# Modulation rows of the first layer's stages: pairs of tiles into one PSUM result

## The reference

```
mod_x = (silu(c) @ w_ada[l] + b_ada[l])[:, None, :]
mod_c =  silu(c_ctx) @ w_ada[l] + b_ada[l]
sh1, sc1, gate1, sh2, sc2, gate2 = split(mod_x, 6)
hx = rms_norm(x, norm_g[l, 0]) * (1.0 + sc1) + sh1     # used from the start of the layer
...                                                     # gate1 .. gate2 are used late in it
```

## Time and profile before

| | us |
|---|---|
| median of the runs (3) | 3360.63 |
| lowest and highest | 3359.15, 3364.89 |
| span of the profiled execution | 3357.8 |
| PE busy in the span | 3114.1 |
| DVE, ACT, POOL busy | 1500.2, 1162.7, 831.6 |

### The profile page before, as it was taken

One profiled execution on the slowest core, in us unless ns is written; L12 is line 12 of the kernel. 1 busy time (PEld: TensorE's weight loads), 2 busy tenths in 40 slices (PEclk: granted clock), 3 DMA queues, 4 the chain that ended last, 5 costly groups with the idle time before them and its releaser, 6 DMA issues.

```text
span 3357.8 us, 79208 instructions
## 1 busy us (share of the span) xinstructions
PE 3114.1 (93%) x34382; PEld 2493.0 (74%) x34382; DVE 1500.2 (45%) x2358; ACT 1162.7 (35%) x2403; POOL 831.6 (25%) x518
## 2 busy tenths in 40 slices
PE   7999898999999998999999888989899989989998
PEld 5777676778777786888888666767667667768886
DVE  4455473745444653100144464756565456330033
ACT  4433333423334424211112353434333345342222
POOL 2211111111123132222223221111111243434453
PEclk9999999999999999999999989999999999999999
DMA  5424242434454441111111233413233343522222
GB/s 212 135 97 145 81 142 101 130 121 144 145 166 151 158 169 57 51 63 62 62 50 63 75 101 98 127 63 120 65 122 106 93 140 115 188 69 95 99 88 75
DMA packets 246714, 364.56 MB, mean 109 GB/s; under 512 B 154080, under 2 KB 155376, under 8 KB 245904
## 3 DMA queue, kind: packets, MB, share of 16 engines
q1 hardware_dynamic: 226976, 294.57, 27.6%
q10 hardware_dynamic: 14976, 35.66, 2.7%
q0 software_dynamic: 4464, 29.92, 2.5%
HBM read 290.88 MB, written 69.21 MB: 107 GB/s over the span
## 4 chain that ended last, share of the span: by engine, by line
PE 76%; DVE 6%; issue 5%; ACT 4%; DMA 2%; DVEq 2%; POOLq 2%; PEld 1%; SPq 1%; POOL 0%; PEldq 0%; ACTq 0%
PE banks L281 20%; PE banks L282 18%; PE banks L283 18%; PE banks L1684 2%; PE banks L1023 2%; PE banks L1695 1%; PE banks L1648 1%; PE banks L395 1%; PE banks L1687 1%; PE banks L1745 1%; POOLq L2430 1%; DVE arena L597 1%; PE banks L2057 1%; PE banks L1051 1%; DMA arena<-chunk_inputs 1%
## 5 line engine op out<-in xcount | busy, mean ns | idle before, releaser
L283 PE MATMUL banks<-hx_rounded,slot_rounded 128*128 128x512 f32 (+1 forms) x1624 | 575.1, 354 | 0.0
L906 POOL TENSOR_TENSOR slot_rounded<-slot,branch_weights_high 128x512 fp32r<-128x512 f32 x188 | 251.4, 1357 | 1286.2 <-ACT branch_weights_high L901 1284.9
L281 PE MATMUL banks<-hx_high,weight_parts 128*128 128x512 f32 (+1 forms) x1512 | 537.9, 356 | 10.9 <-DVE hx_low L545 10.4
L281 PE MATMUL banks<-hx_rounded,branch_weights_high 128*128 128x512 f32 (+1 forms) x1280 | 498.8, 390 | 48.1 <-DVE arena L1364 8.6
L282 PE MATMUL banks<-hx_low,weight_parts 128*128 128x512 f32 (+1 forms) x1512 | 538.0, 356 | 0.0
L283 PE MATMUL banks<-hx_high,weight_parts 128*128 128x512 f32 (+1 forms) x1512 | 535.9, 354 | 0.0
L282 PE MATMUL banks<-resid_rounded,branch_weights_high 128*128 128x512 f32 (+1 forms) x1280 | 452.7, 354 | 0.0
L283 PEld LDWEIGHTS banks<-hx_rounded,slot_rounded 128*128 128x128 f32 x1624 | 312.2, 192 | 44.3
L281 PEld LDWEIGHTS banks<-hx_rounded,branch_weights_high 128*128 128x128 f32 x1280 | 245.9, 192 | 128.2 <-issue 75.6
L281 PEld LDWEIGHTS banks<-hx_high,weight_parts 128*128 128x128 f32 x1512 | 286.6, 190 | 55.1 <-issue 14.3
L283 PEld LDWEIGHTS banks<-hx_high,weight_parts 128*128 128x128 f32 x1512 | 286.3, 189 | 41.1
(11 more groups left out here) (263 smaller groups left out, 5853.7 us busy)
## 6 DMA issues: line engine op xcount, KB each, us to landing
slot<-in_w_mix SPq DMA_DIRECT2D x120, 512.0 KB, 3.9
slot<-in_w_ffn_in SPq DMA_DIRECT2D x88, 512.0 KB, 3.3
arena<-chunk_inputs SPq DMA_DIRECT2D x48, 640.0 KB, 4.5
arena<-in_w_ada SPq DMA_DIRECT2D x50, 512.0 KB, 5.1
slot<-in_w_ffn_out SPq DMA_DIRECT2D x44, 512.0 KB, 3.3
slot<-in_w_ada SPq DMA_DIRECT2D x40, 512.0 KB, 4.3
chunk_inputs<-arena SPq DMA_DIRECT2D x80, 256.0 KB, 3.9
arena<-side_projections POOLq DMA_DIRECT2D x16, 1152.0 KB, 6.1
```

Source lines behind the costliest of these rows:

```text
L281: first = nc.tensor.matmul(out, w_hi, x_hi, start=start, stop=False)
L283: return first, nc.tensor.matmul(out, w_lo, x_hi, start=False, stop=stop)
L906: last = nc.gpsimd.tensor_tensor(slots_r[g % 3][:, half], slots[g % 3][:, half], weights_high(g)[:, half], ALU.subtract)
```

## The change

Two tiles, c and c + 1 with c even, become a pair. `ada_rows` gets two flags, so that the eight matmuls of tile c + 1 accumulate on those of tile c in the same 128 x 128 result of bank 6 (they fill different rows and add zeros to the others). `rows_pe` multiplies both, with a wait for each slab, and signals each buffer. `rows_dve` waits for the second and adds once. `rows_of` returns the even number of a pair, at the projection tile where its odd one stood; so a tile has at most one pair, now after step k = 4, and the planner counts 0.9 for it where it counted 0.5 for each. SP requests the slabs c + 2 and c + 3 together, each after the multiplication of the same buffer's tile. The number of matmuls, DMAs and bytes is unchanged; 40 bank waits and 40 DVE additions are gone.

```diff
-        def ada_rows(slab, out, row=0):
+        def ada_rows(slab, out, row=0, first=True, end=True):
...
-                last = nc.tensor.matmul(out[q, :], CIN[:, k, left:left + 32], slab[:, k * P:(k + 1) * P], start=(k < 4), stop=(k >= 4), skip_group_check=True)
+                last = nc.tensor.matmul(out[q, :], CIN[:, k, left:left + 32], slab[:, k * P:(k + 1) * P], start=first and k < 4, stop=end and k >= 4, skip_group_check=True)
...
-            return [] if l else list(range(before, before + count(TILES[g][0], TILES[g][2])))
+            return [] if l else [c - 1 for c in range(before, before + count(TILES[g][0], TILES[g][2])) if c % 2]
...
-            pe.wait_ge(rows_full[c % 2], c // 2 * 16 + 16)
-            ada_rows(ROWS[c % 2], bank[6][:, 0:P], c % GROUP).then_inc(rows_used[c % 2], 1)
-            banks_of.busy[0] = (ada_taken, c + 1)
+            for b in range(2):
+                pe.wait_ge(rows_full[b], c // 2 * 16 + 16)
+                ada_rows(ROWS[b], bank[6][:, 0:P], c % GROUP + b, b == 0, b == 1).then_inc(rows_used[b], 1)
+            banks_of.busy[0] = (ada_taken, c // 2 + 1)
...
-            dve.wait_ge(rows_used[c % 2], c // 2 + 1)
+            dve.wait_ge(rows_used[1], c // 2 + 1)
...
-                    for c in rows_of(l, g)[(k == 6):(k == 6) + 1] if k in (3, 6) else []:
+                    for c in rows_of(l, g) if k == 4 else []:
...
-                        yield 0.5
+                        yield 0.9
...
-                            if c + 2 < NROWS:
-                                rows_load(sp, c + 2)
+                            for x in (c + 2, c + 3):
+                                if x < NROWS:
+                                    rows_load(sp, x)
```

More of the change, by code:

```diff
@@ L1144, in weight @@
             def weight(t0, t1):
-                return sum(KD * sum(COST[s] for s in tile_segs(l, g0 + t)) + 0.5 * len(rows_of(l, g0 + t)) for t in range(t0, t1))
+                return sum(KD * sum(COST[s] for s in tile_segs(l, g0 + t)) + 0.9 * len(rows_of(l, g0 + t)) for t in range(t0, t1))
             out_cost = sum(COST[s] for s in outs)
@@ L2003, in steps @@
                     at_bank.slot_before = g % 3
-            tile_cost = KD * sum(COST[s] for s in tile_segs(l, NT - 1)) + 0.5 * len(rows_of(l, NT - 1))
+            tile_cost = KD * sum(COST[s] for s in tile_segs(l, NT - 1)) + 0.9 * len(rows_of(l, NT - 1))
             opening = [[tile_cost * x for x in (((1.0, 1.5)[l], 0.6, 0.3) if hp == 0 else (0.5, 0.6, 0.3))] for hp in range(HP)]
```

## The result

The changed kernel takes 3367.66 us (median of 20 runs) against 3360.13 us for the kernel before (20 runs): ratio 1.0021, 95% interval 1.0014 to 1.0027. It is 7.5 us slower. The interval leaves out 1, so the loss is clear of the scatter, but it is as small as the 0.2% within which the prediction speaks of no change. The profiled execution has a span of 3366.2 us, 8.4 above that of before.

What follows compares the result with a forecast made beforehand. PE time was taken as the bound: 3357.8 - 9.4 (PE saving) + 1 (thinned visits) + 9.5 (slab waits) + 3 (clock) = 3361.9 us of span, 3364.7 as median, stated as 3364.5; range 3355 to 3373.

Steps and rivals of the forecast that it cites:

- signs: In the changed trace: time up to 890 us shorter by 4 to 6 us, attention longer by 7 to 10.
- Cost of a pair: On PE, beside chain or unit: first half 0.58 us, second 0.47, between bounds of 0.47 and 0.58.
- Saving before attention: PE time saved by pairs in the stages before attention: 6 of the 9.4 us in all.
- thinned visits: Three visits of each body stage lose their only set, leaving less filler for DVE trips: 1 us lost, between 0 and 3.
- The rival in which the thinned visits swallow the gain: Before attention, thinned visits wait for DVE and ACT, so only attention's saving stays: 3370 us; chance 0.11.
- Waits for slabs: In attention, PE waits at pairs 50, 52, 60 and 68: 12.7 us against 3.17, 9.5 more.
- The rival of quick landings: In attention, close slab requests land after 3.6 and 4.5 us and the clock holds: 3358.2 us; chance 0.12.
- The clock: In attention, PE falls to 1.2 GHz after waits in stages 1 and 3: 3 us lost, bounds 0 and 8.
- the rival of the longer slow clock: In attention, PE stays at 1.2 GHz twice as long after waits of all three stages: some 8 us, 3369.5; chance 0.17.
- DVE at nothing: The 40 additions DVE is spared lie beside PE and earn nothing; without that cover 11.5 us at most.
- that rival: DVE was behind part of PE's waits; all 40 additions on the path bring 11.5 us: 3353 us; chance 0.10.

Runs made afterwards that it cites:

- experiment 1: Kernel before, with pairs only for the 48 tiles before attention and single tiles in attention; 3353.29 us against 3359.88, ratio 0.9975.
- Experiment 6: Changed kernel with 48 matmuls of the identity, their result unread, ahead of the halves that wait for slabs; 3360.22 us, ratio 1.0002 to the kernel before.
- experiment 3: Changed kernel, but in attention a pair is taken only after planned work of at least 4.9 since the last; 3346.36 us, ratio 0.9964 to the kernel before.
- Experiment 5: As experiment 1, but each pair's tiles are two separate sets with own bank wait and DVE addition; 3377.26 us, ratio 1.0052 to the kernel before.

## Why the prediction was right, and where its sizes were off

The forecast was no change, 3364.5 us, with slower at 0.31. Measured was 3367.66, inside the range, and slower by 0.21%, at the bound itself. The mechanism and its places were right, but the closeness of the total is partly luck. Up to tile 78 the forecast has 5 us of gain and 9.1 of loss (-3.4 + 9.5 + 3), that is +4.1; the means of two traces each have 7.8 of gain and 12.0 of loss, +4.2. Both sizes were too small, and both lie outside what I had named as signs (4 to 6 earlier, 7 to 10 longer); the errors cancel.

**Cost of a pair.** Forecast 1.05 us (0.58 + 0.47, the lower bound, for the second half); measured 1.01. The wait between halves is free when the slab is there, as the earlier trace rows suggested.

**Saving before attention.** Forecast 6 us less 1 us for thinned visits; tile 48 starts 7.8 us earlier as a mean of two traces each, and experiment 1 is 6.6 us faster as a whole. By the measured pair, 24 first halves (1 x 0.78 + 23 x 0.58) and 24 second ones of 0.43 make 24.4 us, against 19 x 0.78 + 29 x 0.58 = 31.6 for the singles: 7.2. With the same time at the lower clock the traces say 7.4. The rival in which the thinned visits swallow the gain did not come.

**Waits for slabs.** Forecast 12.7 us at pairs 50, 52, 60 and 68; measured 13.66 at exactly these. Pair 60 was forecast at 3.1 and 0.9 and has 3.12 and 1.14. Pair 68's second half waited 2.54 us, where I had 1.2: its slab took 6.6 us to land. But the term is the difference to before, and there the second trace has 5.6 us, so it is 10.5 or 8.1 us where I had 9.5. The rival of quick landings did not come: for these four pairs the first slab landed 3.3 to 4.9 us after its request, the second 4.7 to 6.6. The estimate of 3.2 us for a slab from the Trainium skill (DMA: Bandwidth & Descriptors, "Anatomy of one DMA — SWDGE (gpsimd) path"), which pointed to it, is fitted to DMAs of the gpsimd path; of these requests in SP's queue only one, with 3.3 us, came near it.

**The clock.** This is the mis-sized term. I took 3 us more than before, with a bound of 8. Experiment 6 measures up to 7.5 us for the changed kernel. The kernel before had one stretch of 3.4 us at half speed, at most 1.7, in one trace and none in the other, so the change adds 6 to 7.5. Stage 2, which I left at its old price, fell for twice as long, and so did the two others. This is the rival of the longer slow clock, to which I gave 0.17; its price of 8 was close to the measured 7.5. By its own words it would decide for slower from 6 us on; that the time stands only at the bound is owed to the larger saving before attention.

**The sum for attention** from the first traces: sets about -4.0 (15 pairs of 1.01 and less switching, an estimate from the steps above), waits +10.5, clock +5.8, together +12.3; the windows say +12.2. With the second trace of before and of the changed kernel: -4.0, +8.1 and +7.5 to 8.0 make 11.6 to 12.1; the windows say +11.8. Taking the waits and the clock away again gives 222.4 - 13.7 - 7.5 = 201.2, and experiment 3, which does that, has 201.5.

**DVE at nothing.** The one place before attention where PE waited for line 885 is the chain's L1731 (L1734 in the changed kernel). PE's waits there, first in the kernel before and then in the changed one:

```profile
PE banks L1731 <- DVE arena L885: 2.2, 3, 0.8
PE banks L1731 <- ACT arena L1196: 0.5, 1, 0.5
```

```profile
PE banks L1734 <- ACT arena L1198: 2.7, 4, 0.7
```

There are four waits of 2.7 us in both, and the second traces agree: where DVE's addition no longer ends the wait, ACT ends it at the same length. So the relief of DVE earned nothing there, as forecast, and this and not only the sum speaks against that rival. Experiment 5 shows the other side: where second sets do wait for DVE to take the first, the kernel is 24 us slower than experiment 1.

Open: the medians differ by 7.5 us, and the means up to tile 78 make 12.0 - 7.8 = 4.2. The other 3 us lie in the last stretch, within its scatter, and no experiment looked for them.

## What to carry to other kernels

When work is merged, the buffers are merged with it: two single buffers that took turns become one that must be empty before it is asked for again. That is free where the items stand far apart and dear where they pile up, so merge first and then spread: the version that did both is 0.36% faster, where the merge alone is 0.21% slower. Price a wait of PE at more than its length: where 13.7 us of waits came in clusters of 4 to 5 us, the slow clock cost another 6.4 to 7.5. And look at what is queued behind a request before it is put off: one late slab request held back the weights, and with them the softmax.

## What had not been expected of the hardware

The clock stayed at its lower level for 6.7 us behind waits of 2.9 us (1.47 + 1.38), 4.3 (3.12 + 1.14) and 4.4 (1.81 + 2.54); in one trace of the kernel before it was down once in attention, for about half of that the earlier trace rows, behind waits of 1.25 and 0.93, and in the other not at all, behind 1.12 and 0.97 and behind a single wait of 2.61. And 11 us of matmuls without use made the kernel 7.6 us faster: they filled waits that were there anyway, and the granted clock stayed at 1.00.
